# Later parameter loads, and two value pages ahead of two row stores, on the SP queue of a one-core decoder layer

## What is computed

```python
z = x @ w_in                                # q, k, v, u, two gates
attn = rms_norm(attend(q, k, v, rel_bias, lam), subln_g) * (1.0 - lam_init)
ssm, s_re, s_im = s5_branch(u, ...)         # state space layer, then g * sigmoid(g @ w_glu)
merged = gate_a * (attn @ w_proj_attn) + gate_s * (ssm @ w_proj_ssm)
h = layer_norm(alpha * x + merged @ w_out, ln1_g, ln1_b)
up = h @ w_up                               # then a causal convolution of width 3 over time
padded = concatenate([conv0, up], axis=1)   # conv0: state_conv of the sample (8, 2, 11008)
c = conv_b + sum(conv_w[j] * padded[:, j:j + seq] for j in range(3))
gate, val = split(c, 2)
y = layer_norm(alpha * h + (silu(gate) * val) @ w_down, ln2_g, ln2_b)
```

## Time and profile before

| | us |
|---|---|
| three executions | 1816.82, 1821.58, 1824.56 |
| median | 1821.58 |
| the profiled execution | 1816.25 |
| its span on the core | 1814.4 |
| PE busy in the span | 1739.6 (96%) |
| DVE, ACT, POOL busy | 1077.3, 644.4, 382.3 |
| mean granted TensorE clock | 0.976 of full |

### The profile page before, as it was taken

How to read it: one execution, slowest core, us unless ns; L and a number is a source line. 1 busy time by engine, 2 the same in 40 slices (tenths; PEclk the granted TensorE clock), 3 DMA queues, 4 the chain that set the end, 5 groups by cost and what they waited for, 6 DMA issues and landing times.

```text
span 1814.4 us, 32580 instructions
## 1 busy us (share of the span) xinstructions
PE 1739.6 (96%) x11922; PEld 1507.4 (83%) x11922; DVE 1077.3 (59%) x1670; ACT 644.4 (36%) x951; POOL 382.3 (21%) x337
## 2 busy tenths in 40 slices
PE   7998999999999998689998999999999999999997
PEld 5786766666666665489997999999999999999995
DVE  1245677767767752467544776766777776444444
ACT  2021334434433412233323544444444443333333
POOL 1034776766676740000000000000000000000000
PEclk9999999999999999899999899999999999999997
DMA  9776999999999976566654466776666658666641
GB/s 214 168 216 209 294 361 341 371 355 353 370 348 331 366 267 196 162 172 184 186 163 116 117 178 172 185 184 172 172 172 171 174 139 220 184 168 185 168 122 48
DMA packets 555635, 393.51 MB, mean 217 GB/s; under 512 B 25666, under 2 KB 504791, under 8 KB 554967
## 3 DMA queue, kind: packets, MB, share of 16 engines
q1 hardware_dynamic: 423376, 325.07, 59.8%
q10 hardware_dynamic: 132160, 67.11, 13.1%
HBM read 385.47 MB, written 7.02 MB: 216 GB/s over the span
## 4 chain that ended last, share of the span: by engine, by line
PE 92%; DMA 3%; SPq 2%; DVE 2%; ACT 1%; POOL 0%; issue 0%; DVEq 0%; ACTq 0%
PE bank L660 26%; PE bank L972 17%; PE bank L973 17%; PE bank L978 17%; PE bank L648 4%; PE bank L628 2%; DMA weight_ring<-in_w_in 2%; PE bank L743 1%; PE bank L732 1%; SPq L474 1%; PE bank L1018 1%; PE bank L758 1%; PE bank L1001 1%; DMA small<-in_ssm_log_dt 0%; DMA work<-in_cache_k 0%; DVE work L1840 0%
## 5 line engine op out<-in xcount | busy, mean ns | idle before, releaser
L660 PE MATMUL bank<-work,weight_ring 128*128 128x264 f32 x2176 | 537.6, 400 | 3.8 <-DMA weight_ring<-in_w_in 3.3
L660 PEld LDWEIGHTS bank<-work,weight_ring 128*128 128x128 f32 x2176 | 409.7, 194 | 119.4 <-issue 53.6
L1353 ACT ACTIVATE weights_hi<-weight_ring 128x2048 fp32r<-128x2048 f32 (+1 forms) x166 | 309.7, 1866 | 549.6 <-PE bank L973 470.6
L1795 DVE TENSOR_TENSOR weights_lo<-weight_ring,weights_hi 128x2048 fp32r<-128x2048 f32 (+1 forms) x166 | 368.9, 2223 | 117.7 <-ACT weights_hi L1353 66.8
L972 PE MATMUL bank<-h_hi,weights_hi 128*128 128x264 f32 x1376 | 345.4, 289 | 8.0 <-DVE h_lo L1851 8.0
L598 POOL TENSOR_TENSOR work<-work 128x512 f32<-128x512 f32 x256 | 319.2, 1276 | 107.2 <-DMA work<-in_cache_k 86.2
L973 PE MATMUL bank<-h_lo,weights_hi 128*128 128x264 f32 x1376 | 340.8, 286 | 0.0
L972 PEld LDWEIGHTS bank<-h_hi,weights_hi 128*128 128x128 f32 x1376 | 260.9, 190 | 11.4 <-issue 8.4
L973 PEld LDWEIGHTS bank<-h_lo,weights_hi 128*128 128x128 f32 x1376 | 261.5, 190 | 0.0
L1632 DVE TENSOR_REDUCE work<-work 128x8 f32<-128x512 f32 x256 | 163.7, 676 | 43.0 <-POOL work L598 42.8
L978 PE MATMUL bank<-h_hi,weights_lo 128*128 128x264 f32 x1376 | 182.2, 285 | 0.0
(11 more groups left out here) (238 smaller groups left out, 1870.5 us busy)
## 6 DMA issues: line engine op xcount, KB each, us to landing
weight_ring<-in_w_up SPq DMA_DIRECT2D x86, 1024.0 KB, 5.7
work<-in_cache_k SPq DMA_DIRECT2D x256, 256.0 KB, 6.6
work<-in_cache_v SPq DMA_DIRECT2D x128, 512.0 KB, 6.6
weight_ring<-in_w_in ACTq DMA_DIRECT2D x60, 1024.0 KB, 12.7
weight_ring<-in_w_down SPq DMA_DIRECT2D x32, 1024.0 KB, 5.9
weight_ring<-in_w_out SPq DMA_DIRECT2D x16, 1024.0 KB, 5.8
weight_ring<-in_w_down SPq DMA_DIRECT2D x16, 704.0 KB, 4.8
weight_ring<-in_w_proj_attn SPq DMA_DIRECT2D x16, 512.0 KB, 4.1
```

The costliest lines, as they stand in the source:

```text
L660: last = pe.matmul(bank[n % 2][:, 0:N], slot(n % SLOTS, k), tiles[k], start=(k == 0), stop=(k == len(tiles) - 1))
L1353: act.activation(w_hi[:, (j % 2) * KT * P:(j % 2) * KT * P + k_tiles * P].bitcast(F32R), slot3(j, 0, k_tiles).rearrange("p k m -> p (k m)" ...
L1795: dve.tensor_tensor(w_lo[:, cols].bitcast(F32R), slot3(off % SLOTS, 0, k_tiles).rearrange("p k m -> p (k m)"), w_hi[:, cols], ALU.subtract ...
```

## The change

The value pages 1 and 2 of sample 7 are issued ahead of the last two row stores. The parameter loads move from behind page 8 to behind page 15, and the three loads of 86 partitions become six: of the first 80 partitions, and of the last 6. PE's waits count the two loads of `state_conv` and the eight on `par_in`.

```diff
             load_values(B - 2, 15)
-            load_values(B - 1, 0)
+            for p in range(3):
+                load_values(B - 1, p)
             store_rows(H - 1, "k_prompt", k_rows, k_stored)
             store_rows(H - 1, "v_prompt", v_rows, v_stored)
-            for p in range(1, PAGES):
+            for p in range(3, PAGES):
                 load_values(B - 1, p)
-                if p == 8:
-                    sp.wait_ge(k_free, 2 * PAGES * B)
-                    sp.dma_start(state_rows[0:2 * FT, :].rearrange("t (r p) -> t r p", p=P),
-                                 a["state_conv"][0].rearrange("b i (t p) -> t (b i) p", p=P)).then_inc(st_in, 16)
...
+            sp.wait_ge(k_free, 2 * PAGES * B)
+            for t0, t1 in ((0, 80), (80, 2 * FT)):
+                sp.dma_start(state_rows[t0:t1, :].rearrange("t (r p) -> t r p", p=P),
+                             a["state_conv"][0].rearrange("b i (t p) -> t (b i) p", p=P)[t0:t1]).then_inc(st_in, 16)
+                sp.dma_start(par_rows[t0:t1, 0:3 * P].rearrange("t (w p) -> t w p", w=3),
+                             a["conv_w"][0].rearrange("w (t p) -> t w p", p=P)[t0:t1]).then_inc(par_in, 16)
+                sp.dma_start(par_rows[t0:t1, 3 * P:4 * P],
+                             a["conv_b"].rearrange("o (t p) -> (o t) p", p=P)[t0:t1]).then_inc(par_in, 16)
+            for n, name in enumerate(("ln1_g", "ln1_b", "ln2_g", "ln2_b")):
...
-            pe.wait_ge(st_in, 16)
-            pe.wait_ge(par_in, 6 * 16)
+            pe.wait_ge(st_in, 2 * 16)
+            pe.wait_ge(par_in, 8 * 16)
```

More of the change, by code:

```diff
@@ L464, in _ @@
             load_values(B - 2, 15)
-            load_values(B - 1, 0)
+            for p in range(3):
+                load_values(B - 1, p)
             store_rows(H - 1, "k_prompt", k_rows, k_stored)
             store_rows(H - 1, "v_prompt", v_rows, v_stored)
-            for p in range(1, PAGES):
+            for p in range(3, PAGES):
                 load_values(B - 1, p)
-                if p == 8:
-                    sp.wait_ge(k_free, 2 * PAGES * B)
-                    sp.dma_start(state_rows[0:2 * FT, :].rearrange("t (r p) -> t r p", p=P),
-                                 a["state_conv"][0].rearrange("b i (t p) -> t (b i) p", p=P)).then_inc(st_in, 16)
[L474 to L480, removed]
+            sp.wait_ge(k_free, 2 * PAGES * B)
[7 more added lines that the diff above has]
+            for n, name in enumerate(("ln1_g", "ln1_b", "ln2_g", "ln2_b")):
+                sp.dma_start(ln_rows[0:KT, n * P:(n + 1) * P],
+                             a[name].rearrange("o (t p) -> (o t) p", p=P)).then_inc(par_in, 16)
             def load_proj(i, split=True):
```

## The result

The changed kernel takes 1799.69 us in the median of 4 executions (1797.79 to 1803.29), the kernel before 1819.2 us in the median of 4 on the same occasion (1815.46 to 1824.56). The ratio is 0.9898, with a 95% interval of 0.9874 to 0.9923: 1.0% faster, clear of the 0.5% that a measurement of this kernel can tell. The forecast was 1797.7 us, in a range of 1791 to 1806. The medians lie 19.5 us apart, where 23.84 us were forecast: 4.3 us of the gain are missing. The time itself lies only 2.0 us off the forecast because the kernel before, on this occasion, was 2.4 us under the median that the forecast started from (1819.2 against 1821.58). That part of the agreement is luck.

What follows compares the result with a forecast made beforehand. PE was taken to bound the kernel, its one large wait caused by SP's queue standing behind one load. Terms 22.05 and 1.79 sum to 23.84 us; 1821.58 - 23.84 = 1797.7 us, range 1791 to 1806.

Steps and rivals of the forecast that it cites:

- What bounded the kernel: PE's 22.05 us wait for value page 9 at line 648 comes from SP's queue standing behind one load.
- Two engines: The 86-partition load uses two DMA engines (share 0.14, 44 GB/s); by the count pattern 80 gives 16, 6 gives six.
- The sum of 23.84 us: Total gain expected from pages 9 to 15 no longer standing behind the parameter loads.
- The two terms, 22.05 and 1.79: At page 9: PE's wait of 22.05 us goes, and the slow restart at low clock, 1.79 us, with it.
- I take 0, because both sums end before 761.05: Parameters behind page 15 land before the transposes start at 761.05, so cost 0, bounded at about 3 us.
- The second sum: Parameter landing with the 1 MB block issued at 718.06 counted in: 3.2 us for it, end at 760.9.
- rival A: Parameters come late: PE waits 1 to 8 us at line 628, 1799 to 1806 us, say 1802; chance 0.10.
- The signs named beforehand: No line 648 page wait above 1 us, clock 1.00, ten loads under 9 us, no 44 GB/s stretch; line 628 waits tell against.
- Pages 1 and 2 ahead of the stores: Issuing these pages of the last sample before the row stores: bounds 0 to 1.5 us earlier issue, taken as 0.
- what follows PE: DVE (44.6 us wait for square roots) and ACT follow PE, so everything behind the stall shifts as a block.
- Rival B: Split does not spread the load; parameters land 19.8 us after PE asks, gain 2.2 us, 1819.4 us; chance 0.04.
- Rival C: Large piece runs on one engine: 39.8 us wait at line 628, 17.8 us slower, 1839.3 us; chance 0.03.

Runs made afterwards that it cites:

- the early version: Against the change, the ten split parameter loads stand ahead of value page 3: 1792.79 and 1793.98 us, ratios 0.9852 and 0.9862 to the kernel before.
- the change third: The changed kernel measured a third time, no edit: 1801.83 us, ratio 0.9885 to the kernel before.
- the change again: The changed kernel measured once more, no edit: 1801.67 us, ratio 0.9885 to the kernel before.
- the projection held back: Against the change, SP waits until all parameters have landed before issuing the first projection blocks: 1798.72 us, ratio 0.9883 to the kernel before.

## Why the prediction was right, and where it was off

- **What bounded the kernel.** Right. The 22.05 us were the queue standing behind one load: the split alone removes all but 2.32 us of them.
- **Two engines.** Right. The pattern read from counts of 8, 86 and 128 held for 79 (a share of 0.07) and for 80 (1.20). That the six-partition pieces use six engines is shown by no row.
- **The sum of 23.84 us.** The two terms, 22.05 and 1.79, were right to the digit: the early version has exactly this stretch. The change itself kept 19.11, 22.52 and 20.92 us of it in its three profiled executions.
- **"I take 0, because both sums end before 761.05".** This is the step that failed. The parameters were to be there 8.9 to 12.1 us after page 15 left SP, and PE to ask after 12.2; it took 12.6 us (729.33 to 741.93), and 1.22 us more until PE went on. The second sum was nearly right; the mistake was to call a margin of 0.15 us (760.9 against 761.05) in time and to leave out the landing, which I had set beside it. The engines were full in the change, a DMA share of 1.12 and 292 GB/s in 729 to 742, but the wait stayed when the blocks behind the parameters were held back. So rival A came about in its mildest form, a wait of 1.2 to 1.5 us, below the 3 us that I had named as the upper bound. The time alone could not have told: 1799.69 lies in the forecast's own span (1793.0 to 1800.7) and in that of rival A (1799 to 1806).
- **What I left out.** A short wait can cost clock. I priced rival A by the wait alone; in the first profiled execution 3.27 us of matmuls at a low clock followed 1.47 us of waiting, in the second none. I had read this very effect behind the long wait, and did not carry it over to the short one. With both, the late parameters cost 4.73, 1.32 and 2.92 us of the stretch in the three profiled executions (71.35, 67.94 and 69.54 against the 66.62 of the early version), where I had put 0.
- **The signs named beforehand.** No wait of a value page, ten loads issued in 8.5 us and no stretch at 44 GB/s came as named. A clock of 1.00 up to the last `w_in` block did not, in two of three executions, and the wait at the transposes was the sign of rival A.
- **Pages 1 and 2 ahead of the stores, and what follows PE.** Taken at 0 and found at 0 within what the profiles can tell.
- **Rival B.** Its price could be measured with the load unsplit, which is the same two engines: unsplit at the new place is 14.6 to 18.0 us slower than the change in the stretch (85.93 against 71.35 to 67.94). I had the wait at 19.8 us, it is 15.47: SP was held 3.4 us less, and from the last issue to PE's start it took 0.9 us less. The Trainium skill, "DMA: Bandwidth & Descriptors", section "Rules for kernel authors", advises against two transfers to disjoint partition halves. Here the two pieces beat the single load by about 0.7% (0.9962 against 0.9885 to 0.9898), as the single one did not use all engines; for loads of 128 partitions no run here shows it.
- **Rival C.** Its price was 17.8 us slower with a wait of 39.8 us; made with 79 partitions it is 33.11 us of waiting and 0.65% slower, 9.6 us between the medians.

## What to carry to other kernels

When a queue stands still in the issue of a DMA, look at the outermost count of the DMA in front of it and at the DMA share in a quiet stretch: a share of 2 sixteenths means two engines. Cut such a load so that the large piece has a multiple of 16 partitions (here 80 of 86), and put it where the queue has a gap and where nothing urgent stands behind it. Here the cut was worth nearly all: the early place without it left a stretch of 82.76 us, the cut in the old place 69.02, both together 66.62. A load that must be there at a fixed time needs margin against the full engines, since a wait of 1.5 us was once followed by three more of slow clock.

## What I had not expected of the hardware

- One partition decides between 22 GB/s (79 partitions) and 309 GB/s (80).
- The load on few engines is itself issued in 0.34 us (79 and 86 partitions); it is the next one on the queue that SP stands in, for 32.93 and 19.36 us.
- After a wait of 1.2 to 2.4 us at the transposes the granted clock fell to 0.50 in three of five executions (the change, the change third, the stores in their old place), and stayed at 1.00 in two (the change again, the projection held back). Where PE did not wait there, in both early executions, it stayed at 1.00. A wait of 2.32 us for page 9 (split, behind page 8) was followed by no fall, one of 3.85 us for page 13 (behind page 12) by 0.50. Why it differs is open: the kernel also shows stretches of low clock where PE had waited no more than 0.3 us, as 370 to 372 us in the profile after, at 0.50.
- Between the last parameter's landing, as the chain gives it, and PE's start lay 1.22 us, where after a value page it was 0.04 us (736.61 + 3.42 = 740.03, and PE at 740.07). The cause was not tried.
